# Chains between engines cut into hops one or two rows apart, and a sigmoid made by tanh

## The chip, the cores and the metric

The kernel runs on one core of a Trainium2 chip. The metric is device time in microseconds (us) of one execution. The engines are TensorE (PE), VectorE (DVE), ScalarE (ACT), GpSimd (POOL, which issues the gathers) and SyncE (SP, which issues the plain loads).

## What is computed

A decoder trunk of two layers on 256 tokens of width 1024, all in fp32. Layer 0 mixes with dilated attention (8 heads) and a spatial gating unit (SGU), layer 1 with an S5 state-space layer and a GLU. Each layer ends with PEER: every token picks 8 x 16 = 128 experts of 16384 and adds up their outputs.

```python
h = rmsnorm(x, norm_mix_g[layer])
x = x + hybrid_ab(...)            # layer 0: attention and SGU, one projection in, one out
x = x + s5_block(...)             # layer 1; its end:
    out = g * jax.nn.sigmoid(g @ glu_w + glu_b)        # g = gelu(y), y from the scan of the states
h = rmsnorm(x, norm_ffn_g[layer])
x = x + peer(...)
    sc = einsum('thpc,pkc->thpk', q, subkeys)          # q = h @ wq; top 16 of 128, twice; top 16 of 256 pairs
    act = gelu(einsum('td,tkd->tk', xb, u_tab[ib]))
    y = einsum('tk,tkd->td', gate * act, v_tab[ib])
return rmsnorm(x, final_norm_g)
```

## The kernel before

The 256 tokens are two tiles of 128 (t = 0, 1), one token on each partition. The expert work is 512 rows g: 2 layers x 2 tiles x 128 experts of each token. A row gathers for each of 128 tokens one expert's u and v (8 KB a token, 1 MB a row) into one of RING = 8 buffers. Then dot_product (VectorE, L1189) multiplies u with h and sums; weights (ScalarE, L572 to L578) takes the Gelu of two rows' dots, multiplies them with their gates and writes two diagonal matrices; expert (TensorE, L813) adds the diagonal times v into PSUM. POOL may gather row g once expert(g - 8) is done (L395 to L399). Rows are counted in groups of 16 (n = g // 16), a group for each head, tile and layer; a slot (n, s) is row 16 n + s.

All other work is put between these rows. There is no scheduler: each engine has its own program, made from the same lists. PRELUDE comes ahead of row 0; between() (L80 to L134) puts stages into slots of WORK; LAST comes after row 511. In row g every engine first runs its own functions of that name for the stages in the slot, then its expert work: VectorE a step of the router in the slots of ROUTE and dot_product(g), ScalarE gate_exp in slot EXP_AT and weights(g - 1) in odd rows, TensorE expert(g - 2) and expert(g - 1) in even rows. Each engine executes strictly in its order, and a function waits on semaphores of the engines it reads from. A stage such as q_turn has a function for TensorE (four transposes, L619) and one for VectorE (copy of the result, L974), and both stand in the same slot.

What is put there: query(n, slot, phase, b) makes queries and scores of two heads (q_mm: eight products of 512 columns, L627; q_in: ScalarE copies them, L468; q_turn; q_score: four products with the keys on TensorE, L734, and ScalarE's copy, L478); the second tile's attention, SGU and output projection in groups 1 to 3; the norms (norm, norm_T); for each tile in layer 1 the S5 layer, 16 pairs five rows apart (s5), then s5_end, gate_T and glu. In s5 VectorE makes for each pair the products with the tables of cosines and sines (L1050, L1051), two sums, four scans (L1059) and two more products (L1062, L1063). The tables are made once for two pairs: turn_counts on ScalarE (L500, L502), fraction on VectorE (L1037), tables on ScalarE (L509 to L513). The router of the next group takes five steps, route_keys to route_gate. The functions of Sqrt, Exp, Sin, Sigmoid and the tanh form of Gelu need table loads on ScalarE between them (ACT_TABLE_LOAD rows). SP issues the loads of weights in its own fixed order; each waits until the last product on its buffer is counted in w_used.

## Time and profile before

| what | us |
|---|---|
| median of 3 runs | 1711.5 |
| lowest and highest | 1708.9, 1713.86 |
| the profiled execution | 1707.23 |
| its span, first to last instruction | 1705.5 |
| TensorE busy | 1372.2 (80%) |
| VectorE busy | 1141.1 (67%) |
| ScalarE busy | 671.5 (39%) |
| POOL busy | 567.9 (33%) |
| moved by the transfers | 607.18 MB, mean 356 GB/s |

All views are of the profiled execution, and their times are counted from its first instruction. A busy share says how much of the time an engine computed, not whether it set the pace; for that one reads which wait ended last in each stretch. The dots of row 0 begin at 107.4 us, the first S5 pair of tile 0 at 577 us and of tile 1 at about 989 us.

### The profile page before, as it was taken

The page shows a single profiled execution, that of the slowest core. Times are in us where ns is not written, and L with a number is a line of the kernel's source. Part 1 is how long each engine was busy: PE and PEld are TensorE (multiplying, and loading weights), DVE is VectorE, ACT ScalarE, POOL GpSimd, SP SyncE. Part 2 cuts the span into 40 slices and gives each one's busy share as a digit, 9 for nine tenths or more (in the row PEclk, how much of TensorE's full clock was granted, in tenths as well). Part 3 has the DMA queues.
Part 4 walks back from the last instruction along what each step waited for, and adds up shares of the span by engine and source line. Part 5 has one row for each costly group of instructions (what it writes and reads, how often), then busy time and mean ns, then how long its engine had stood idle before and what let it go on. Part 6 is the DMA issues. An engine that isn't in the chain of part 4 may idle for free.

```text
span 1705.5 us, 14417 instructions
## 1 busy us (share of the span) xinstructions
PE 1372.2 (80%) x3816; PEld 638.7 (37%) x3816; DVE 1141.1 (67%) x2821; ACT 671.5 (39%) x1833; POOL 567.9 (33%) x517
## 2 busy tenths in 40 slices
PE   7997878688797588888878778888978977777776
PEld 3543433233343244444334334444434433222222
DVE  3347563566765799999465589999846556666764
ACT  2224332333333555554243365555334333333332
POOL 0024222233343243444233334333414335434341
PEclk9999889899899798998999989988989999999999
DMA  9479788799899789999999968999989889999996
GB/s 360 174 270 389 290 353 303 304 344 399 334 418 417 286 346 385 360 378 369 373 365 399 384 264 337 366 369 374 371 343 373 341 313 420 421 421 422 422 421 263
DMA packets 106401, 607.18 MB, mean 356 GB/s; under 512 B 9296, under 2 KB 9424, under 8 KB 40784
## 3 DMA queue, kind: packets, MB, share of 16 engines
q0 software_dynamic: 73728, 536.90, 78.9%
q1 hardware_dynamic: 32592, 69.37, 11.1%
q8 instruction: 30, 0.49, 0.1%
q14 instruction: 51, 0.42, 0.1%
HBM read 605.19 MB, written 1.05 MB: 355 GB/s over the span
## 4 chain that ended last, share of the span: by engine, by line
PE 38%; DVE 28%; DMA 17%; DVEq 6%; ACT 6%; issue 4%; ACTq 1%; POOL 0%; POOLq 0%
PE ps L813 23%; DMA rings<-in_uv_tab_dram,idx 16%; PE ps L627 13%; DVE rings L1189 12%; DVE mem L1059 2%; ACT dgs L578 2%; DVEq L1052 1%; ACT wgt L575 1%; DVE mem L1062 1%; DVE mem L1050 1%; PE ps L619 1%; DVEq L1067 1%; DVE mem L1051 1%; ACT gel L572 1%; ACTq L576 1%
## 5 line engine op out<-in xcount | busy, mean ns | idle before, releaser
L813 PE MATMUL ps<-rings,dgs 128*128 128x512 f32 x2048 | 1002.5, 641 | 277.9 <-ACT dgs L578 277.8
L397 POOL DMA_INDIRECT rings<-in_uv_tab_dram,idx x512 | 566.6, 1107 | 1072.4 <-PE ps L813 985.8
L1189 DVE CUSTOM_DVE_ANT_0 rings<-rings,h 128x1024 f32<-128x1024 f32 x512 | 610.9, 1222 | 156.6 <-DMA rings<-in_uv_tab_dram,idx 143.3
L813 PEld LDWEIGHTS ps<-rings,dgs 128*128 128x128 f32 x2048 | 403.5, 204 | 825.5 <-issue 442.2
L572 ACT ACTIVATE gel<-dots 128x2 f32<-128x2 f32 x256 | 52.0, 203 | 651.5 <-DVE dots L1189 651.4
L578 ACT ACTIVATE dgs<-cst,wgt 128x128 f32<-128x128 f32 x512 | 177.6, 394 | 18.8 <-issue 1.4
L627 PE MATMUL ps<-wst,hT 128*128 128x512 f32 x384 | 171.1, 593 | 0.0
L575 ACT ACTIVATE wgt<-gel,share 128x1 f32<-128x1 f32 x512 | 123.0, 287 | 18.0 <-issue 0.3
L974 DVE COPY mem<-ps 128x512 f32<-128x512 f32 x16 | 11.1, 691 | 151.2 <-PE ps L619 151.2
L627 PEld LDWEIGHTS ps<-wst,hT 128*128 128x128 f32 x384 | 72.9, 190 | 92.5 <-issue 91.0
L572 ACT ACT_TABLE_LOAD x60 | 77.0, 1283 | 11.7 <-DVE dots L1189 10.1
L777 PE MATMUL ps<-mem 128*128 128x32 f32 x512 | 62.7, 277 | 0.0
L777 PEld LDWEIGHTS ps<-mem 128*128 128x128 f32 x512 | 59.9, 192 | 5.3 <-issue 1.9
L627 PE MATMUL ps<-rings,hT 128*128 128x512 f32 x128 | 58.5, 608 | 2.0 <-DVE scr L877 1.2
L468 ACT ACTIVATE mem<-ps 128x512 f32<-128x512 f32 x16 | 9.6, 597 | 121.8 <-PE ps L627 121.8
L1189 DVE DVE_READ_ACCUMULATOR2_ANT dots<- 128x1 f32 x512 | 42.0, 82 | 0.0
L559 ACT ACT_TABLE_LOAD x32 | 41.1, 1283 | 0.6
L627 PEld LDWEIGHTS ps<-rings,hT 128*128 128x128 f32 x128 | 24.4, 196 | 31.0 <-issue 30.9
L859 DVE TENSOR_TENSOR x<-x,ps 128x512 f32<-128x512 f32 x12 | 7.9, 683 | 40.3 <-PE ps L627 35.0
L1111 DVE TENSOR_TENSOR mem<-ps,vec 128x512 f32<-128x512 f32 x4 | 2.8, 691 | 42.6 <-PE ps L627 42.6
L1059 DVE TENSOR_TENSOR_SCAN mem<-s5s,z_init,mem 128x128 f32<-128x128 f32 x64 | 25.8, 464 | 1.8 <-issue 0.4
L734 PE MATMUL ps<-sk,mem 128*128 128x128 f32 x128 | 18.2, 286 | 9.4 <-DVE mem L974 9.4
(174 smaller groups left out, 924.4 us busy)
## 6 DMA issues: line engine op xcount, KB each, us to landing
wst<-in_wq_dram SPq DMA_DIRECT2D x15, 2048.0 KB, 10.6
wst<-in_w_out_dram SPq DMA_DIRECT2D x4, 2048.0 KB, 17.2
rings<-in_uv_tab_dram,idx POOLq DMA_INDIRECT x512, 9.6
wst<-in_glu_w_dram SPq DMA_DIRECT2D x4, 2048.0 KB, 22.8
rings<-in_w_in_dram SPq DMA_DIRECT2D x3, 2048.0 KB, 16.6
vec<-in_vecs_dram SPq DMA_DIRECT2D x11, 512.0 KB, 9.0
rings<-in_w_in_dram SPq DMA_DIRECT2D x2, 1024.0 KB, 8.6
dgs<-in_w_in_dram SPq DMA_DIRECT2D x1, 2048.0 KB, 19.4
```

The source lines that it names most:

```text
L397: nc.gpsimd.indirect_dma_start(out=ring[:, g % RING, :], out_offset=None, in_=uv_tab, in_offset=bass.IndirectOffsetOnAxis(ap=idx[n % 4][:, ...
L559: A.activation(gexp[n % 2][:, :], cs[n % 2][:, :], ACT.Exp, bias=ncs[n % 2][:, :], accum_out=gsum[n % 2][:, :]).then_inc(exp_ok, 1)
L572: A.activation(gel[i][:, every], dots[i][:, every], ACT.Gelu_apprx_tanh)
L575: A.activation(wgt[i][:, c], gel[i][:, c], ACT.Copy, scale=share[i][:, c])
L576: act.drain()
L578: A.activation(diag[:, (g + k) % DIAGS, :], ident, ACT.Copy, scale=wgt[i][:, c]).then_inc(diag_ok, 1)
L627: ins = PE.matmul(ps[:, bank, :], lhs[:, k, :], rhs[:, k, :], start=(k == 0), stop=(k == KC - 1))
L734: ins = PE.matmul(ps[:, 2, a * P:(a + 1) * P], qT[:, a, :], sk[:, p // T, a % 2, :], start=True, stop=True)
L777: ins = PE.matmul(o, d, m[:, j, v, :], start=(q == 0), stop=(q == 3))
L813: ins = PE.matmul(ps[:, 4 + 2 * t + b, :], diag[:, g % DIAGS, :], ring[:, g % RING, D + b * BANK:D + (b + 1) * BANK], start=(g % (PH * TOP ...
L1059: V.tensor_tensor_scan(zst[:, i, r, :], dec[:, tile:tile + 1].to_broadcast([P, P]), by_cos[:, i, r, :], z_init[:, r, tile:tile + 1] if t e ...
L1189: V.tensor_tensor_reduce(out=u, in0=u, in1=h[:, t, :], scale=1.0, scalar=0.0, op0=ALU.mult, op1=ALU.add, accum_out=dots[n % 2][:, s:s + 1] ...
```

## The change

Every stage that ran over several engines in one slot is cut at each change of engine, and the parts stand one or two rows apart: query now takes eight rows (q_in one row behind the last product, then q_turn, q_copy, q_score, q_keep), norm six, attention seven. w_out and glu are issued in parts of three or four products (w_mm, glu_mm) as the query's were. Scores go into PSUM bank 3 instead of 2, so that queries can stand five rows apart (slots 107 + 5 b) and overlap. s5 becomes s5_mm, s5_rot, s5_turns, s5_scan and s5_tables in five rows that follow one another; fraction moves to the end of s5_scan. The router's steps and gate_exp move by one slot. y_sum of a tile moves from slot 4 to slot 2. The Sqrt on a spare value ahead of each norm stays only in the prelude. The sigmoid is (1 + tanh(x / 2)) / 2: Tanh on ScalarE, and the 1 and the 0.5 go into the two operations of VectorE that were there. Ring, gathers, dot_product, weights and expert stay as they are.

```diff
 DIAGS = 16
-ROUTE = {2: "route_keys", 4: "route_pairs", 6: "route_best", 8: "route_index", 10: "route_gate"}
-EXP_AT = 8
+ROUTE = {3: "route_keys", 5: "route_pairs", 7: "route_best", 9: "route_index", 11: "route_gate"}
+EXP_AT = 9
 S5_TILES = 32
 RMS_EPS, LN_EPS = 1e-6, 1e-5
...
     def query(n, slot, phase, b):
         at(n, slot, ("q_mm", phase, b, 0, 3))
         at(n, slot + 1, ("q_mm", phase, b, 3, 6))
-        at(n, slot + 2, ("q_mm", phase, b, 6, 8), ("q_in", phase, b))
-        at(n, slot + 3, ("q_turn", phase, b))
-        at(n, slot + 4, ("q_score", phase, b))
-
-    at(0, 0, ("z_out", 6), ("z", 7, 0, 8), ("z_out", 7), ("z", 8, 0, 8), ("z_out", 8), ("z", 9, 0, 8), ("z_out", 9))
-    at(0, 4, ("qk_turn", 1))
+        at(n, slot + 2, ("q_mm", phase, b, 6, 8))
+        at(n, slot + 3, ("q_in", phase, b))
+        at(n, slot + 4, ("q_turn", phase, b))
+        at(n, slot + 5, ("q_copy", phase, b))
+        at(n, slot + 6, ("q_score", phase, b))
+        at(n, slot + 7, ("q_keep", phase, b))
+
+    def norm(n, slot, m):
+        for i, name in enumerate(("norm_sq", "norm_ms", "norm_sd", "norm_h", "norm_T", "hT_copy")):
+            if m < 8 or i < 4:
+                at(n, slot + i, (name, m))
+
+    def product(n, slot, name, *which):
+        at(n, slot, (name, *which, 0, 3))
+        at(n, slot + 1, (name, *which, 3, 6))
+        at(n, slot + 2, (name, *which, 6, 8))
+
+    def attention(n, slot, a):
+        for i, name in enumerate(("att_scores", "att_max", "att_exp", "att_den", "att_pT", "att_pT_copy", "att_o")):
+            at(n, slot + i, (name, a))
+
+    at(0, 0, ("z_out", 6), ("z", 7, 0, 8), ("z", 8, 0, 8), ("z", 9, 0, 8), ("z_out", 7), ("z_out", 8), ("z_out", 9))
+    at(0, 2, ("qk_turn", 1))
+    at(0, 3, ("qkT_copy", 1))
     query(0, 6, 0, 1)
-    at(1, 1, ("sgu_a", 1))
-    at(1, 4, ("att_a", 1))
-    at(1, 6, ("att_b", 1))
-    query(1, 10, 0, 2)
-    at(2, 2, ("att_a", 2))
-    at(2, 4, ("att_b", 2))
-    at(2, 6, ("sgu_b", 1))
-    at(2, 9, ("mix", 1))
-    at(2, 11, ("mix_T", 1))
-    at(2, 13, ("w_out", 1, 0))
-    at(3, 2, ("w_out", 1, 1))
-    at(3, 6, ("norm", 3))
-    at(3, 9, ("norm_T", 3))
-    query(3, 11, 0, 3)
-    query(4, 3, 1, 3)
+    at(1, 1, ("sgu_var", 1))
+    at(1, 2, ("sgu_sd", 1))
+    at(1, 3, ("sgu_norm", 1))
+    at(1, 4, ("sgu_mm", 1))
+    at(1, 5, ("sgu_gate", 1))
+    attention(1, 6, 1)
+    query(1, 13, 0, 2)
+    attention(2, 6, 2)
+    at(2, 14, ("mix", 1))
+    at(2, 15, ("mix_T", 1))
+    at(3, 0, ("mixT_copy", 1))
+    product(3, 1, "w_mm", 1, 0)
+    at(3, 4, ("w_sum", 1, 0))
+    product(3, 4, "w_mm", 1, 1)
+    at(3, 7, ("w_sum", 1, 1))
+    norm(3, 8, 3)
+    query(3, 14, 0, 3)
+    query(4, 4, 1, 3)
     at(5, 2, ("s5_angle",))
     query(5, 8, 1, 0)
     at(6, 2, ("s5_setup",))
     query(6, 9, 1, 1)
-    query(7, 6, 1, 2)
+    query(7, 5, 1, 2)
     for t in range(T):
         g = PH * (t + 1)
-        at(g, 4, ("y_sum", 2 + 2 * t), ("norm", 4 + 2 * t))
-        at(g, 7, ("norm_T", 4 + 2 * t))
+        at(g, 2, ("y_sum", 2 + 2 * t))
+        norm(g, 3, 4 + 2 * t)
         for pair in range(S5_TILES // 2):
-            at(g, 10 + 5 * pair, ("s5", t, pair))
-        at(g, 92, ("s5_end", t))
-        at(g, 94, ("gate_T", t))
-        at(g, 95, ("glu", t, 0))
-        at(g, 99, ("glu", t, 1))
-        at(g, 103, ("norm", 5 + 2 * t))
-        at(g, 106, ("norm_T", 5 + 2 * t))
-        query(g, 108, 2 + t, 0)
-        query(g, 114, 2 + t, 1)
-        query(g, 120, 2 + t, 2)
-        query(g, 128, 2 + t, 3)
-    at(24, 4, ("y_sum", 6), ("norm", 8))
+            slot = 9 + 5 * pair
+            at(g, slot, ("s5_mm", t, pair))
+            at(g, slot + 1, ("s5_rot", t, pair))
+            at(g, slot + 2, ("s5_turns", t, pair))
+            at(g, slot + 3, ("s5_scan", t, pair))
+            at(g, slot + 4, ("s5_tables", t, pair))
+        at(g, 89, ("s5_last", t))
+        at(g, 90, ("s5_sum", t))
+        at(g, 91, ("s5_gelu", t))
+        at(g, 92, ("gate_T", t))
+        at(g, 93, ("gT_copy", t))
+        for b in range(2):
+            at(g, 94 + 2 * b, ("glu_mm", t, b, 0, 4))
+            at(g, 95 + 2 * b, ("glu_mm", t, b, 4, 8))
+            at(g, 96 + 2 * b, ("glu_bias", t, b))
+            at(g, 97 + 2 * b, ("glu_sig", t, b))
+            at(g, 98 + 2 * b, ("glu_sum", t, b))
+        norm(g, 101, 5 + 2 * t)
+        for b in range(4):
+            query(g, 107 + 5 * b, 2 + t, b)
+    at(24, 2, ("y_sum", 6))
+    norm(24, 3, 8)
     return work
...
-            def norm(m):
+            def warm():
+                A.activation(sq_warm[:, :], half_pi, ACT.Sqrt)
+
+            def norm_sq(m):
                 t = NORM_T[m]
                 if m < 2:
                     act.wait_ge(ld_x[t], 16)
                 else:
-                    A.activation(sq_warm[:, :], half_pi, ACT.Sqrt)
                     act.wait_ge(x_done, 2 * (m - 1))
                 A.activation(h[:, t, :], x[:, t, :], ACT.Square, accum_out=ss[:, t:t + 1]).then_inc(sq_done, 1)
+
+            def norm_sd(m):
+                t = NORM_T[m]
                 act.wait_ge(ms_done, m + 1)
                 A.activation(sd[:, t:t + 1], ms[:, t:t + 1], ACT.Sqrt).then_inc(sd_done, 1)
...
-            def q_score(p, b):
+            def q_keep(p, b):
...
-                A.activation(S[:, cols, :], ps[:, 2, :].rearrange("p (a s) -> p a s", a=2),
+                A.activation(S[:, cols, :], ps[:, 3, :].rearrange("p (a s) -> p a s", a=2),
                              ACT.Copy).then_inc(s_act, 1)
...
-            def s5(t, pr):
+            def s5_mm(t, pr):
+
+                if pr == 0:
+                    act.wait_ge(hT_act, 5 + 2 * t)
+                    turn_counts(KC * t)
+                    tables(KC * t)
+
+            def s5_turns(t, pr):
 
                 c = pr // 2
                 ci = KC * t + c
                 if pr % 2:
-                    if c + 1 < KC:
-                        tables(ci + 1)
...
+            def s5_tables(t, pr):
+
+                if pr % 2 and pr + 1 < 16:
+                    tables(KC * t + pr // 2 + 1)
...
-            def glu(t, b):
+            def glu_sig(t, b):
                 act.wait_ge(bias_ok, 2 * t + b + 1)
                 g = gate[:, b * BANK:(b + 1) * BANK]
-                A.activation(g, g, ACT.Sigmoid).then_inc(sig_ok, 1)
+                A.activation(g, g, ACT.Tanh, scale=0.5).then_inc(sig_ok, 1)
...
 
-            def w_out_(t, b):
-                pe.wait_ge(mT_act, t + 1)
-                pe.wait_ge(mT_dve, t + 1)
-                banks_2_3()
-                stream(2 + b, t, WOUT_USE[t] + b)
+            def w_mm(t, b, k0, k1):
+                if k0 == 0:
+                    pe.wait_ge(mT_act, t + 1)
+                    pe.wait_ge(mT_dve, t + 1)
+                    banks_2_3()
+                stream(2 + b, t, WOUT_USE[t] + b, k0, k1)
 
             def q_mm(p, b, k0, k1):
                 if k0 == 0:
...
                 turn(3, qs, qt_done)
+                moved["qs"] = (qs_act, k + 1)
 
             def q_score(p, b):
 
                 pe.wait_ge(qt_dve, k + 1)
                 pe.wait_ge(ld_sk, 16)
                 for a in range(4):
-                    ins = PE.matmul(ps[:, 2, a * P:(a + 1) * P], qT[:, a, :], sk[:, p // T, a % 2, :], start=True, stop=True)
+                    ins = PE.matmul(ps[:, 3, a * P:(a + 1) * P], qT[:, a, :], sk[:, p // T, a % 2, :], start=True, stop=True)
                 ins.then_inc(s_done, 1)
                 moved["scores"] = (s_act, k + 1)
 
...
+            def s5_scan(t, pr):
+
+                c, js, cos, sin, by_cos, by_sin = s5_views(pr)
...
+                V.tensor_tensor(by_cos, zst, cos, ALU.mult).then_inc(d_ok, 1)
+                V.tensor_tensor(by_sin, zst, sin, ALU.mult).then_inc(d_ok, 1)
...
+                dve.drain()
                 if pr % 2 and pr + 1 < 16:
-                    fraction(ci + 1)
-                s5_pair(t, pr)
-
-            def s5_end(t):
+                    fraction(KC * t + c + 1)
+
...
+            def glu_sum(t, b):
+                cols = slice(b * BANK, (b + 1) * BANK)
                 dve.wait_ge(sig_ok, 2 * t + b + 1)
-                V.tensor_tensor(gate[:, cols], gate[:, cols], h[:, t, cols], ALU.mult)
-                dve.drain()
-                residual(t, b, gate[:, cols])
+                V.scalar_tensor_tensor(gate[:, cols], gate[:, cols], 1.0, h[:, t, cols], ALU.add, ALU.mult)
+                dve.drain()
+                xs = x[:, t, cols]
+                V.scalar_tensor_tensor(xs, gate[:, cols], 0.5, xs, ALU.mult, ALU.add).then_inc(x_done, 1)
```

## Rows read from the trace of the kernel before

**Rows 1.** The page: transfers in 40 equal slices of the span

```profile
...
DMA  9479788799899789999999968999989889999996
GB/s 360 174 270 389 290 353 303 304 344 399 334 418 417 286 346 385 360 378 369 373 365 399 384 264 337 366 369 374 371 343 373 341 313 420 421 421 422 422 421 263
```

**Rows 2.** Windows: length; PE, PEld, DVE, ACT, POOL busy (count); clock, DMA share, GB/s

```profile
...
107.40:571.60 464.20, 363.15 (x920) 167.71 (x919) 275.65 (x708) 159.85 (x440) 150.53 (x138) 0.92 0.91 359
...
603.00:809.90 206.90, 180.61 (x621) 92.31 (x620) 194.88 (x490) 106.26 (x298) 84.97 (x73) 0.90 0.93 366
809.90:984.10 174.20, 142.84 (x373) 66.06 (x372) 93.81 (x232) 61.35 (x158) 52.29 (x48) 0.95 0.97 380
...
1015.90:1233.00 217.10, 186.75 (x650) 95.63 (x649) 201.18 (x483) 108.79 (x306) 86.19 (x76) 0.91 0.92 363
1233.00:1413.10 180.10, 149.82 (x366) 67.40 (x364) 97.87 (x242) 65.09 (x171) 57.63 (x51) 0.93 0.91 346
1413.10:1691.00 277.90, 205.44 (x445) 80.09 (x446) 184.31 (x456) 94.00 (x301) 110.22 (x107) 1.00 1.00 417
```

**Rows 3.** Waits, whole span: us in total, times, longest one

```profile
...
POOL rings L397 <- PE ps L813: 985.8, 451, 16.0
...
DVE mem L974 <- PE ps L619: 151.2, 16, 13.4
...
ACT mem L468 <- PE ps L627: 121.8, 16, 13.4
...
DVE mem L1111 <- PE ps L627: 42.6, 4, 12.3
```

**Rows 4.** Timelines of VectorE, ScalarE, TensorE around one query: start, us, what, idle before

```profile
...
369.96 0.69 DVE L974 COPY mem<-ps 128x512 f32<-128x512 f32 x1 [12.35 <-PE ps L619]
...
368.61 0.60 ACT L468 ACTIVATE mem<-ps 128x512 f32<-128x512 f32 x1 [13.36 <-PE ps L627]
...
358.11 5.31 PE L627 MATMUL ps<-wst,hT 128*128 128x512 f32 x12
363.26 3.60 PE L813 MATMUL ps<-rings,dgs 128*128 128x512 f32 x8
```

**Rows 5.** Timeline of TensorE in the stretch of gathers alone, two experts

```profile
...
1669.17 3.70 PE L813 MATMUL ps<-rings,dgs 128*128 128x512 f32 x8 [1.26 <-ACT dgs L578]
```

**Rows 6.** Waits of VectorE from 620 to 780 us, inside the first S5 stretch

```profile
...
DVE rings L1189 <- DMA rings<-in_uv_tab_dram,idx: 1.4, 2, 1.2
```

**Rows 7.** Timelines of ScalarE and VectorE inside the first S5 stretch

```profile
...
678.70 0.20 ACT L572 ACTIVATE gel<-dots 128x2 f32<-128x2 f32 x1 [1.15 <-DVE dots L1189]
...
680.24 1.28 ACT L509 ACT_TABLE_LOAD   x1
681.53 0.63 ACT L509 ACTIVATE mem<-mem 128x512 f32<-128x512 f32 x1
...
682.75 0.72 ACT L512 ACTIVATE mem<-mem,cst 128x512 f32<-128x512 f32 x1
...
685.60 1.22 DVE L1189 CUSTOM_DVE_ANT_0 rings<-rings,h 128x1024 f32<-128x1024 f32 x1
...
686.75 1.22 DVE L1189 CUSTOM_DVE_ANT_0 rings<-rings,h 128x1024 f32<-128x1024 f32 x1
```

**Rows 8.** Timeline of VectorE at the first S5 pair

```profile
...
577.42 0.69 DVE L1037 SCALAR_TENSOR_TENSOR mem<-mem 128x512 f32<-128x512 f32 x1 [3.45 <-ACT mem L502]
580.74 0.69 DVE L1050 TENSOR_TENSOR mem<-ps,mem 128x512 f32<-128x512 f32 x1 [2.63 <-ACT mem L512]
```

**Rows 9.** Timeline of VectorE, start of route_best and the dot behind it

```profile
...
370.56 0.42 DVE L1146 MAX8 cs<-cand_a 128x8 f32<-128x256 f32 x1
...
373.35 1.23 DVE L1189 CUSTOM_DVE_ANT_0 rings<-rings,h 128x1024 f32<-128x1024 f32 x1
```

**Rows 10.** Timeline of ScalarE at the end of the kernel

```profile
...
1700.27 0.19 ACT L413 ACTIVATION_READ_ACCUMULATOR h<-x 128x1 f32 x1
1700.67 0.20 ACT L415 ACTIVATE sd<-ms 128x1 f32<-128x1 f32 x1 [0.22 <-DVE ms L844]
```

More of the change, by code:

```diff
@@ L520, in s5 @@
                 if pr % 2:
-                    if c + 1 < KC:
-                        tables(ci + 1)
                     return
-                if c == 0:
-                    act.wait_ge(hT_act, 5 + 2 * t)
-                    turn_counts(ci)
-                    tables(ci)
-                    if t == 0:
-                        act.wait_ge(ld_c, 16)
-                        act.wait_ge(cz_zero, 2)
+                if c == 0 and t == 0:
+                    act.wait_ge(ld_c, 16)
+                    act.wait_ge(cz_zero, 2)
                 if c + 1 < KC:
@@ L684, in att_b, with att_o @@
                     turn(2 + i, E[i], pT_done)
+                moved["pT"] = (pT_act, 2 * a + 2)
+            def att_o(a):
+                t, units = att_units(a)
                 for i, (h0, nh) in enumerate(units):
```

144 lines of the change are left out of this document (80 added, 64 removed).

## The prediction

> **What bounds the kernel now.** I read the 40 slices first, then the windows by stretch, then the waits, then the timelines. The main loop is 512 rows, and each row gathers 1 MB. In the last stretch the chip moves 417 GB/s at a DMA share of 1.00, and single slices show 421 or 422 [rows 1, 2]. Nothing but gathers and expert work is left there, so this is the ceiling of the transfers. Everywhere else one asks what keeps the kernel below it. The windows split the loop into two kinds. The two S5 stretches (603.0 to 809.9 and 1015.9 to 1233.0) have VectorE busy for 194.9 of 206.9 us and 201.2 of 217.1 us, and in 160 us of the first VectorE waited only 1.4 us for gathered rows [rows 2, 6]: VectorE is the bound, its small gaps are bubbles. The three other stretches have VectorE at 54 to 59%, TensorE at 78 to 83%, and the transfers at 359, 380 and 346 GB/s [rows 2]: no engine is full, and waits across engines are what costs. The waits name them: POOL waits 985.8 us for TensorE to free a ring buffer, VectorE waits 151.2 us in 16 places for a transposed query, ScalarE 121.8 us for the same 16 query products, VectorE 42.6 us in 4 places for the GLU products [rows 3].
>
> **Why those waits reach the transfers.** Before, the stages of a chain stand in one row or in two neighbouring ones of every engine's order. TensorE's work of a row stands ahead of the experts of the two rows before, so it is late by some rows. A VectorE that has reached the row stands still until TensorE comes. The query at 358 shows it: VectorE idles 12.35 us for the transpose; ScalarE idles 13.36 us before it copies the product, and so holds back the weights of dots that were finished when VectorE fell idle (369.96 - 12.35 = 357.6); TensorE needs 5.31 us for six of the eight products and 3.60 us for two experts in between [rows 4]. With no new weights no expert runs, no buffer is freed, no gather starts.
>
> **Part 1, the stretches outside S5.** Moved by the gathers' ceiling, the bytes of the three stretches (464.2 x 359, 174.2 x 380, 180.1 x 346) would take 396, 157 and 148 us, 117 us less than they do. By the DMA share (0.91, 0.97, 0.91) they were idle for 42, 5 and 16 us, together 63. The first counts the less efficient weight loads as loss, the second misses half-empty queues. I take the middle, 90 us, as what could be recovered. How much is? In the free rhythm a row takes 2.5 us, and two experts 3.70 us on TensorE [rows 2, 5]. For a query that starts in an even row, take the end of the dot of the row before as zero. TensorE is free at about 0; three products (2.65 us), a pair of experts (3.7), three products, the last two (1.9) put the end of q_mm at about 11 us, the next pair's at 14.5 and the transpose's near 15.3. ScalarE, whose next weights need the dot that ends at 10, copies the product then: late by about 1 us instead of idling 7.6 (121.8 / 16). VectorE gets to q_copy at 12.5 and waits about 3 us instead of 9.4 (151.2 / 16). What lasts is TensorE itself: a query is 7.2 us of products and some 2 us of transposes and scores, in 5 rows that leave 12.5 - 5 x 1.85 = 3.2 us. Where four queries stand 5 rows apart (slots 107 to 129) TensorE is the local bound at (5 x 1.85 + 9.2) / 5 = 3.7 us a row, and the 2 MB of weights of each query cost the transfers nearly as much. y_sum moves from slot 4 to slot 2, where the last experts of the tile are just finished, and can wait some us behind such a cluster, three times. So I take three quarters of the 90, **68 us**; the ends are a third (30), if these clusters rule, and all of the high figure (117).
>
> **Part 2, the first S5 pair of each tile.** Before, VectorE waits 3.45 us for turn_counts and 2.63 us for tables [rows 8]. After, ScalarE makes the counts one row ahead, and its table load too. What remains is about 2 us of Sin, Abs and Sin, so 2 x (3.45 + 2.63 - 2) = **8 us** for both tiles; the price is that the weights of slots 8 and 9 stand behind that row of ScalarE, ends 0 and 12.
>
> **Part 3, the later S5 tables.** This one goes the other way. Before, ScalarE makes the next tables in the row where VectorE first makes the fraction and then a whole pair and five dots, so nobody waits. Now the fraction stands at the end of s5_scan (slot + 3), tables at slot + 4, and the s5_rot that reads them at the next slot + 1, only three dots on. The slots with tables are 14, 24 ... 74, all even, so slot + 3 is odd and ScalarE first makes the weights of that row, which need its dot. From the start of that dot: 1.23 until its result, 0.1, weights 1.54 (678.70 to 680.24), table load 1.29, Sin, Abs, Sin 1.94: 6.1 us. VectorE is there after three dots of 1.15, at 3.45 [rows 7]. That is a stall of 2.65 us on the engine that is the bound, seven times a tile, 18.6. A router step between the dots hides some: route_best (373.35 - 370.56 = 2.8 us [rows 9]) one whole stall, route_keys and route_pairs by their sizes about 1.7 each, route_gate 0.4. That leaves 18.6 - 2.65 - 3.4 - 0.4 = 12 a tile, **24 us lost**. The ends are 0 (VectorE is itself held up elsewhere) and 14 x (2.65 + 3.6) = 87 us: the weights of the next pair are queued behind the tables and a reload, TensorE's experts wait for them 3.6 us longer (until 7.4 instead of 3.8), and that is added if it starves the ring as well. The split of the pair itself adds no instruction, and I cost it at nothing, since VectorE has its landed rows anyway.
>
> The Trainium skill (page "ScalarE: Activation LUTs", section "What ACT_TABLE_LOAD costs") puts a switch at about 2.66 us, load and drain together. Here Sin starts 0.01 us after a load of 1.28 us ended [rows 7], so the trace disagrees and the row decides; by the page the stalls would be 1.4 us longer each and the sum 19 us worse.
>
> **Part 4, small edits.** The prelude has the same order on each engine; its rows cost nothing. The warm Sqrt goes, except once: its load moves to norm_sd. In the loop the count of loads stays. At the end it was made while ScalarE waited for the last sum, now it stands between Square and Sqrt (1700.46 to 1700.67), and costs 1.28 - 0.21 = **1.1 us** [rows 10]. Sigmoid by Tanh removes up to 8 table loads of 1.28 us if Tanh is in the set of the Gelu, none if not; both are beside TensorE's product, so 0, ends 0 and 5 gained. Scores in bank 3 let the next product start early: part of the 68. The router one row later: the index is still ready before the expert whose buffer that gather takes, nothing. Attention, SGU and norms in hops belong to part 1. SP's queue keeps its order; its loads wait for w_used and h_done and come earlier or later with them.
>
> **Sum.** -68 - 8 + 24 + 1 = -51 us. Against the profiled execution's 1707.2 us that is 1656; the median of the three runs is 4.3 us above the profiled one, so the forecast is 1711.5 - 51, **1660 us**.
>
> **The rivals.** (B) The transfers become the bound nearly everywhere and VectorE's S5 stalls are half as large: -90 - 8 + 12 + 1 = -85, **1626 us**. For it: the stretch from 1413 runs at 417 GB/s as soon as no chains cross. (C) One row is too short a distance: TensorE is late by two rows in the clusters, so every hop is a wait again, and only 40% of 90 returns: -36 - 8 + 24 + 1 = -19, **1692 us**. For it: TensorE at 83% of the last such stretch; against: a row there is 3.3 us, which leaves more room. (D) Slower: tables in S5. If a table costs the full 6.25 us, then -68 - 8 + 87 + 1 = +12, **1723 us**; it decides from (68 + 8 - 1) / 14 = 5.4 us a table. For it: a DVE-bound stretch pays every wait in full; against: the ring holds eight rows. (E) The change doesn't decouple: engines meet later in the same order and wait as long, **1711 us**. Against: TensorE's late row is one or two rows late, as the pairs of experts in the query's rows show, and the new distances are as long. (F) A table switch costs about twice its load (14 x 1.4 us of further stall): 19 us on top of the forecast, **1679 us**; the trace speaks against it [rows 7]. That is what the Trainium skill's rule above would give.
>
> **Chances.** Forecast 0.50, B 0.18, C 0.19, D 0.06, E 0.05, F 0.02. Within 0.3% (5 us) is what a measurement of this kernel can't tell from no change. Faster 0.90, same 0.04, slower 0.06. The forecast's own range is 1640 to 1680; the wide one goes from 1615 (all of B) to 1700 (all of C).
>
> **What would show it.** In the profile after: VectorE's wait for the transpose before q_copy falls from 9.4 us to about 3 each; the share of the transfers in the first stretch rises to about 0.97; the S5 stretches stay as long or get some 8 us longer each, with a new VectorE wait for the Sin of tables, 2 to 3 us in about five of seven rows; a table load before the last Sqrt. The prediction is wrong if S5 itself gets shorter (then VectorE wasn't the bound), or if POOL's wait for TensorE stays near 986 us with TensorE busy throughout (then TensorE was).

## The result and the profile after

| what | us |
|---|---|
| before, median of 4 runs on the same chip | 1710.44 |
| after, median of 4 runs (lowest, highest) | 1660.04 (1657.36, 1663.61) |
| ratio after / before, 95% interval | 0.9704 (0.9680 to 0.9728) |
| the profiled execution of after, and its span | 1663.61, 1661.6 |

The change is 50.4 us faster by the medians; the two profiled executions are 43.6 us apart, since the profiled one of after is the slowest of its four. The forecast was 1660, with a range of 1615 to 1700.

The first view is again the page's slices of transfers, which [rows 1] show for before.

```profile
...
DMA  9569799999799999888999999989899899999996
GB/s 360 188 254 400 315 377 368 407 393 391 324 400 417 366 370 343 333 348 347 384 412 367 413 363 359 340 311 343 355 385 399 315 402 421 422 421 421 413 414 257
```

Outside S5 the slices are fuller: the seventh to ninth have 368, 407 and 393 where before had 303, 304 and 344. The ceiling is where it was, 421 to 422. The windows by stretch (length; PE, PEld, DVE, ACT, POOL busy with counts; clock, DMA share, GB/s) are cut at the dots of rows 0, 136, 146, 218, 264, 274, 348, 400 and 511, as in [rows 2].

```profile
...
107.40:535.90 428.50, 354.36 (x917) 163.19 (x915) 274.36 (x699) 151.12 (x430) 152.59 (x138) 0.93 0.96 380
535.90:565.00 29.10, 21.26 (x75) 10.55 (x76) 25.29 (x56) 18.16 (x52) 8.74 (x8) 0.82 0.88 345
565.00:789.40 224.40, 187.62 (x642) 94.16 (x641) 198.89 (x500) 114.09 (x311) 83.27 (x75) 0.92 0.91 353
789.40:942.90 153.50, 135.81 (x350) 62.70 (x348) 88.68 (x222) 52.54 (x145) 49.26 (x46) 0.93 0.99 392
942.90:971.70 28.80, 20.91 (x75) 10.40 (x76) 26.28 (x59) 17.21 (x47) 10.82 (x8) 0.82 0.87 352
971.70:1202.00 230.30, 189.61 (x651) 95.64 (x650) 203.29 (x493) 115.62 (x313) 88.20 (x77) 0.92 0.90 347
1202.00:1367.30 165.30, 144.79 (x365) 65.26 (x363) 97.93 (x243) 60.05 (x169) 58.42 (x53) 0.96 0.95 375
1367.30:1646.70 279.40, 212.04 (x446) 83.54 (x447) 184.76 (x456) 93.92 (x301) 111.38 (x107) 0.97 1.00 415
```

VectorE's work in the first line is what it was (274.4 against 275.7 us busy), so nearly all of the 35.7 us that went was time in which it stood idle; TensorE's idle time fell by 27 us there. In the S5 lines VectorE's busy time grew by 4.0 and 2.1 us while the lengths grew by 17.6 and 13.2 us.

The same stretches for the kernels that follow, in us, each read off the dots of its own trace. Each line is one execution. Up to row 136 after, e1, e2, e6 and e11 are the same program, and there they have 421.5 to 432.7 us; in the first cluster (218-264) e6 and e11, the same program up to the last row, have 152.1 and 145.4. So a difference of less than some 10 us in the first column, or 7 in a cluster, says little by itself:

| kernel | 0-136 | 136-146 | S5 146-218 | 218-264 | 264-274 | S5 274-348 | 348-400 | 400-511 | last dot to end |
|---|---|---|---|---|---|---|---|---|---|
| before | 464.2 | 31.4 | 206.8 | 174.2 | 31.8 | 217.1 | 180.2 | 278.3 | 14.1 |
| after | 428.5 | 29.2 | 224.4 | 153.5 | 28.8 | 230.3 | 165.3 | 279.4 | 14.9 |
| e3, S5 hops alone | 465.1 | 28.1 | 217.3 | 173.9 | 28.3 | 227.8 | 180.1 | 278.1 | 14.1 |
| e4, query hops alone | 463.2 | 31.4 | 206.7 | 165.7 | 31.9 | 215.9 | 167.7 | 278.5 | 14.1 |
| e5, all but S5 and query hops | 439.0 | 32.5 | 214.6 | 156.1 | 32.8 | 220.0 | 168.9 | 278.7 | 14.9 |
| e2, all but S5 hops | 432.7 | 32.6 | 214.4 | 157.6 | 32.9 | 218.8 | 168.9 | 279.3 | 14.9 |
| e1, after with early fraction | 425.1 | 29.0 | 212.3 | 151.5 | 29.2 | 218.5 | 166.7 | 279.1 | 14.9 |
| e6, e1 with last query later | 428.0 | 28.6 | 213.2 | 152.1 | 28.8 | 217.7 | 158.0 | 279.2 | 14.9 |
| e10, e6 with the copy a row later | 425.9 | 28.5 | 211.7 | 148.7 | 28.8 | 217.5 | 158.3 | 277.9 | 14.9 |
| e11, e6 with the Sqrt ahead of the end | 421.5 | 28.5 | 212.6 | 145.4 | 29.1 | 217.6 | 159.8 | 277.0 | 13.8 |
| e12, all that helped | 422.0 | 28.7 | 211.8 | 144.3 | 29.5 | 217.7 | 158.1 | 279.0 | 13.8 |

The waits of after over the whole span (engine, line, waited for: us in total, times, longest):

```profile
...
POOL rings L434 <- PE ps L869: 942.8, 459, 19.9
...
DVE rings L1264 <- DMA rings<-in_uv_tab_dram,idx: 173.5, 132, 4.3
...
DVE mem L1041 <- PE ps L668: 104.0, 16, 16.3
...
ACT mem L510 <- PE ps L676: 89.9, 16, 13.5
...
DVE mem L1182 <- PE ps L676: 32.4, 4, 10.2
...
DVE mem L1137 <- issue: 24.1, 12, 2.6
...
PE ps L676 <- DMA wst<-in_wq_dram: 12.8, 2, 7.8
```

The waits of [rows 3] are smaller, not gone: VectorE's for the transposed query 104.0 us instead of 151.2, ScalarE's for the query's product 89.9 instead of 121.8, VectorE's for GLU's product 32.4 instead of 42.6. Two are new: VectorE 12 times at L1137 (the first product with the tables) for 24.1 us, and TensorE twice for weights of a query. Eleven of the twelve, 22.8 us, stand in the two S5 stretches at tables that come late; the twelfth, 1.28 us at 950.86, is at the first pair of the second tile. Here is one of the twelve, in timelines of ScalarE and VectorE from 596 us (start, us, what, idle before):

```profile
...
597.36 0.20 ACT L620 ACTIVATE gel<-dots 128x2 f32<-128x2 f32 x1 [4.65 <-DVE dots L1264]
...
598.89 1.28 ACT L551 ACT_TABLE_LOAD   x1
600.18 0.63 ACT L551 ACTIVATE mem<-mem 128x512 f32<-128x512 f32 x1
...
601.40 0.72 ACT L554 ACTIVATE mem<-mem,cst 128x512 f32<-128x512 f32 x1
...
602.21 0.69 DVE L1137 TENSOR_TENSOR mem<-ps,mem 128x512 f32<-128x512 f32 x1 [2.60 <-issue]
```

ScalarE makes the weights of the odd row first (597.36), then loads the table, then makes the Sin; VectorE starts its product 0.1 us after the last Sin ends and has stood still for 2.60 us. The profile puts the wait down to "issue"; that it is the Sin is seen by setting the two engines side by side, and e1 tests it.

### The profile page after: what moved, and what is told of

It is laid out like the page before. It is cut to its first block and busy times, and to the rows that moved or that the text cites. A ratio compares the mean times of both kernels' runs of the same rounds, so it can differ in the third digit from the quotient of the medians.

```text
span 1661.6 us, 14475 instructions
## 1 busy us (share of the span) xinstructions
PE 1366.6 (82%) x3816; PEld 634.4 (38%) x3816; DVE 1142.9 (69%) x2821; ACT 654.3 (39%) x1814; POOL 568.5 (34%) x517
## 5 line engine op out<-in xcount | busy, mean ns | idle before, releaser
L1264 DVE CUSTOM_DVE_ANT_0 rings<-rings,h 128x1024 f32<-128x1024 f32 x512 | 615.5, 1224 | 190.3 <-DMA rings<-in_uv_tab_dram,idx 173.5
L620 ACT ACTIVATE gel<-dots 128x2 f32<-128x2 f32 x256 | 52.0, 203 | 684.5 <-DVE dots L1264 684.1
L676 PE MATMUL ps<-wst,hT 128*128 128x512 f32 x384 | 176.6, 606 | 14.5 <-DMA wst<-in_wq_dram 12.8
L1041 DVE COPY mem<-ps 128x512 f32<-128x512 f32 x16 | 11.1, 692 | 104.0 <-PE ps L668 104.0
L620 ACT ACT_TABLE_LOAD x54 | 69.3, 1283 | 1.7
L510 ACT ACTIVATE mem<-ps 128x512 f32<-128x512 f32 x16 | 9.6, 597 | 89.9 <-PE ps L676 89.9
L1137 DVE TENSOR_TENSOR mem<-ps,mem 128x512 f32<-128x512 f32 x32 | 22.0, 689 | 26.4 <-issue 24.1
L607 ACT ACT_TABLE_LOAD x30 | 38.5, 1283 | 0.7
L918 DVE TENSOR_TENSOR x<-x,ps 128x512 f32<-128x512 f32 x12 | 7.9, 684 | 36.9 <-PE ps L676 24.6
L1182 DVE TENSOR_TENSOR mem<-ps,vec 128x512 f32<-128x512 f32 x4 | 2.8, 692 | 32.4 <-PE ps L676 32.4
## 6 DMA issues: line engine op xcount, KB each, us to landing
wst<-in_glu_w_dram SPq DMA_DIRECT2D x4, 2048.0 KB, 23.7
rings<-in_w_in_dram SPq DMA_DIRECT2D x3, 2048.0 KB, 16.6
```

The lines of the kernel that those rows point to most:

```text
L607: A.activation(gexp[n % 2][:, :], cs[n % 2][:, :], ACT.Exp, bias=ncs[n % 2][:, :], accum_out=gsum[n % 2][:, :]).then_inc(exp_ok, 1)
L620: A.activation(gel[i][:, every], dots[i][:, every], ACT.Gelu_apprx_tanh)
L676: ins = PE.matmul(ps[:, bank, :], lhs[:, k, :], rhs[:, k, :], start=(k == 0), stop=(k == KC - 1))
L1041: V.tensor_copy(qT, four(3)).then_inc(qt_dve, 1)
L1137: V.tensor_tensor(by_cos, x4, cos, ALU.mult)
L1264: V.tensor_tensor_reduce(out=u, in0=u, in1=h[:, t, :], scale=1.0, scalar=0.0, op0=ALU.mult, op1=ALU.add, accum_out=dots[n % 2][:, s:s + 1] ...
```

## The experiments

**e1: the fraction early, the tables two rows earlier.** It tells whether the waits for late tables cost their full length, and whether they are the distance's fault.

```diff
-            at(g, slot + 4, ("s5_tables", t, pair))
+            at(g, slot + 2, ("s5_tables", t, pair))
...
             def s5_rot(t, pr):
...
+                if pr % 2 and pr + 1 < 16:
+                    fraction(KC * t + c + 1)
...
             def s5_scan(t, pr):
...
-                if pr % 2 and pr + 1 < 16:
-                    fraction(KC * t + c + 1)
```

> The changed kernel with one thing moved: fraction goes from the end of s5_scan to the end of s5_rot (odd pairs), and s5_tables from slot + 4 to slot + 2, so that ten rows lie between the tables and the s5_rot that reads them. Theory (part 3 of the prediction: VectorE is the bound in S5 and each late table costs 2.6 us): the 12 waits before the first product of s5_rot (24.1 us after the change) go, and the time falls by 20 to 24 us, to 1636 to 1640. Rival (the waits only took the place of other idle time, since transfers and the ring would have held VectorE up anyway): the waits go, waits for gathered rows come in their place, and the time falls by less than 8 us.

Measured: 1636.62 us, 0.9578 (0.9550 to 0.9607) of before, 23.4 less than after. The eleven waits for late tables are gone; what is left is the one at the first pair of the second tile, whose tables the edit doesn't touch:

```profile
...
DVE mem L1137 <- issue: 1.3, 1, 1.3
```

The windows of its S5 stretches:

```profile
...
562.70:775.00 212.30, 177.12 (x640) 90.70 (x639) 198.10 (x500) 109.66 (x307) 88.12 (x74) 0.95 0.94 370
...
955.70:1174.20 218.50, 183.12 (x653) 93.62 (x652) 202.89 (x491) 110.97 (x308) 89.14 (x77) 0.95 0.94 365
```

They are 12.1 and 11.8 us shorter with VectorE nearly as busy as in after: 22.8 us of waits for tables and 1.6 us that it stands less at s5_sum, against 23.9 us of time. The waits for gathered rows that the rival expected in their place did not come (170.7 us over the span, 173.5 in after). In S5 these waits of VectorE cost their whole length.

**e2: the hops of S5 taken back, the rest of the change kept.** The five stages of a pair stand in one slot again, with the fraction ahead of the pair.

```diff
-            at(g, slot, ("s5_mm", t, pair))
...
-            at(g, slot + 4, ("s5_tables", t, pair))
+            for name in ("s5_mm", "s5_rot", "s5_turns", "s5_scan", "s5_tables"):
+                at(g, 10 + 5 * pair, (name, t, pair))
```

> The changed kernel with the S5 pairs put back into one row each (slot 10 + 5 per pair; fraction ahead of the pair, tables beside it), everything else as changed. Theory (the split of a pair is worth nothing, only its tables cost): the first pair of each tile costs about 4 us more again and the late tables are gone, so 8 us above the kernel with the early fraction: 1644 to 1648, and 12 to 16 us below the changed kernel. Rival (two short visits of VectorE instead of one long one help the ring): well above the kernel with the early fraction, 1655 or more.

Measured: 1649.47 us, 0.9645 (0.9610 to 0.9680); its profiled execution was the longest of four, 1661.09. By the median it is 10.6 us faster than after: the hops of S5, as the change has them, lose time. It is 12.9 us slower than e1, which has the hops of after with an early fraction. So the hops are worth something once the fraction isn't late: in the profiles the stretches 136-146 and 264-274, with the first pair in them, are 3.6 and 3.7 us shorter in e1. The rest lies mostly outside S5, in rows where the two are the same program, so it isn't shown that the hops give it.

**e3: the hops of S5 alone, on the kernel before.**

```diff
-            at(g, 10 + 5 * pair, ("s5", t, pair))
+            slot = 9 + 5 * pair
+            at(g, slot, ("s5_mm", t, pair))
...
+            at(g, slot + 4, ("s5_tables", t, pair))
```

> The kernel before with only the S5 pairs in hops, as the changed kernel has them; queries, norms, attention, GLU as before. Theory: slower than before by the sum of parts 2 and 3, 24 - 8 = 16 us, 1724 to 1730. Rival (hops in S5 gain, and the changed kernel's long S5 stretches come from something else, such as the router one row later): 1711 or less.

Measured: 1721.91 us, 1.0074 (1.0046 to 1.0103), 13.8 slower than the 1708.12 of before beside it, a little less than the theory's 16. Of its waits, the one at its first product with the tables:

```profile
...
DVE mem L1081 <- issue: 23.7, 12, 2.6
```

Twelve waits for late tables, six in each tile, without anything else of the change. By stretch: +10.5 and +10.7 in S5, -3.3 and -3.5 at the first pairs, together +14.4. That is parts 2 and 3 of the prediction measured alone (it had -8 and +24).

**e4: the hops of the queries alone, on the kernel before** (with scores in bank 3 and the first query of a cluster at slot 107).

```diff
-        at(n, slot + 2, ("q_mm", phase, b, 6, 8), ("q_in", phase, b))
-        at(n, slot + 3, ("q_turn", phase, b))
-        at(n, slot + 4, ("q_score", phase, b))
+        at(n, slot + 2, ("q_mm", phase, b, 6, 8))
+        at(n, slot + 3, ("q_in", phase, b))
+        at(n, slot + 4, ("q_turn", phase, b))
+        at(n, slot + 5, ("q_copy", phase, b))
+        at(n, slot + 6, ("q_score", phase, b))
+        at(n, slot + 7, ("q_keep", phase, b))
```

> The kernel before with only the queries in hops (eight rows, scores in bank 3), started in the slots of before (the first of a cluster one slot earlier, because its scores must be kept in time); norms, attention, output projection, GLU and S5 as before. Theory (queries' waits were 151 of the about 280 us that VectorE waited outside S5): about half to two thirds of the gain of the stretches outside S5 (85 us by the marks of the rows), 40 to 55 us, 1655 to 1670. Rival (the gain came from the norms, attention and y_sum around them): under 20 us, above 1690.

Measured: 1683.55 us, 0.9848 (0.9819 to 0.9877), 24.6 us faster than before, between what the theory (40 to 55) and the rival (under 20) expected. Its wait for the transposes:

```profile
...
DVE mem L980 <- PE ps L623: 78.5, 14, 13.7
```

72.7 us of waits are gone, and the stretches give -8.5 and -12.5 in the two clusters and only -1.0 in rows 0 to 136, where seven of the 15 queries stand. It fits that the chains of attention, SGU and norms, still in one row each, held the engines up there anyway (e5).

**e5: all but the hops of S5 and of the queries** (e2, with each query in its five rows of before, and the clusters at 108, 114, 120, 128; the slots of y_sum and the router, and Tanh, are those of after).

```diff
-        at(n, slot + 2, ("q_mm", phase, b, 6, 8))
-        at(n, slot + 3, ("q_in", phase, b))
-        at(n, slot + 4, ("q_turn", phase, b))
-        at(n, slot + 5, ("q_copy", phase, b))
-        at(n, slot + 6, ("q_score", phase, b))
-        at(n, slot + 7, ("q_keep", phase, b))
+        at(n, slot + 2, ("q_mm", phase, b, 6, 8), ("q_in", phase, b))
+        at(n, slot + 3, ("q_turn", phase, b), ("q_copy", phase, b))
+        at(n, slot + 4, ("q_score", phase, b), ("q_keep", phase, b))
...
-            query(g, 107 + 5 * b, 2 + t, b)
+            query(g, (108, 114, 120, 128)[b], 2 + t, b)
```

> The kernel with S5 pairs in one row, and the queries too put back to five rows and to their old slots (scores stay in bank 3): so only attention, SGU, output projection, norms, GLU and y_sum are in hops. Queries alone gave 25 us, and S5 in one row with all others in hops gave 59. Theory (parts add up, since the stalls stand in different rows): 1708 - (59 - 25) = 1674, 1669 to 1680. Rival (they overlap: a stall taken away in a row only pays once its neighbour is gone too): either half alone gives less than its share, 1685 or more.

Measured: 1663.56 us, 0.9746 (0.9724 to 0.9769), 43.6 us faster than before, more than either theory gave it. Its wait for the transposes is nearly that of before (151.2 us):

```profile
...
DVE mem L1034 <- PE ps L661: 147.0, 16, 16.4
```

So 43.6 us can be had while the waits that the prediction put first are all there. Queries alone give 24.6 and the others alone 43.6, 68.2 in sum, and e2, which has both, gives 58.7: they overlap, mostly in the clusters (218-264: -8.5, -18.1 and together -16.6; 348-400: -12.5, -11.3 and together -11.3). There each edit takes part of what the other would; it isn't a last bound, since e12 gets to 144.3 and 158.1. In rows 0 to 136 it is the other way round: -1.0 and -25.2 alone, together -31.5 in e2 and -35.7 to -42.7 in after, e1, e6 and e11, which are the same program there. So the queries' hops pay in those rows only once the other chains are cut.

**e6: e1 with the last query of a cluster three rows later.**

```diff
-            query(g, 107 + 5 * b, 2 + t, b)
+            query(g, (107, 112, 117, 125)[b], 2 + t, b)
```

> The kernel with the early fraction, and the fourth query of each cluster starts in slot 125 instead of 122. Theory (the waits of 13 to 16 us for its transpose come from weights that land 30 us after their issue, for which TensorE waited 7.8 us in one cluster and 5.1 in the other): TensorE's wait for the weights goes, and 5 to 12 us fall off, 1625 to 1632. Rival (TensorE or the transfers are full over the whole cluster, so the wait only moves): within 3 us of 1637.

Measured: 1627.81 us, 0.9529 (0.9502 to 0.9556), 8.8 us less than e1. What it is aimed at, in after's timelines of TensorE and VectorE in the first cluster:

```profile
...
877.30 2.74 PE L676 MATMUL ps<-wst,hT 128*128 128x512 f32 x6
...
900.28 5.30 PE L676 MATMUL ps<-wst,hT 128*128 128x512 f32 x6 [7.75 <-DMA wst<-in_wq_dram]
...
918.11 0.69 DVE L1041 COPY mem<-ps 128x512 f32<-128x512 f32 x1 [16.31 <-PE ps L668]
```

The load of these weights is issued at 870.18 and takes 30.0 us to land; TensorE stands 7.75 us for it, and VectorE 16.31 us for the transpose behind it. The wait costs TensorE more than its length: the six matmuls behind it take 5.30 us where six took 2.74 just before, and from 900.28 to 904 the granted clock is 0.50, the lower of its two levels (1.2 GHz), after TensorE had stood idle. In e6 the waits, whole span:

```profile
...
DVE mem L1041 <- PE ps L668: 92.0, 16, 12.5
...
PE ps L676 <- DMA wst<-in_wq_dram: 5.1, 1, 5.1
```

In this execution the second cluster is 8.7 us shorter than in e1, and the first isn't: there TensorE now waits 5.1 us for the weights of the third query. It isn't so in every execution: in e11, the same program up to the last row, TensorE waits for no weights, and both clusters are shorter than in e1, by 6.1 and 6.9 us. The medians, 1627.81 and 1622.10 against 1636.62, leave no doubt of the gain.

**e7: Sigmoid in place of Tanh,** on the kernel after.

```diff
-                A.activation(g, g, ACT.Tanh, scale=0.5).then_inc(sig_ok, 1)
+                A.activation(g, g, ACT.Sigmoid).then_inc(sig_ok, 1)
...
-                V.scalar_tensor_tensor(gate[:, cols], gate[:, cols], 1.0, h[:, t, cols], ALU.add, ALU.mult)
+                V.tensor_tensor(gate[:, cols], gate[:, cols], h[:, t, cols], ALU.mult)
```

> The changed kernel with the sigmoid as before (Sigmoid on ScalarE, product and sum as two plain operations). Theory (part 4: the 8 or so table loads stand beside TensorE's product): four loads for Sigmoid and as many for the Gelu come back, the time stays within 3 us of 1660. Rival (each load delays the weights in rows where VectorE waited 10 and 6 us for the GLU product, so both halves pay): 5 to 10 us more, 1665 to 1670.

Measured: 1658.70 us, 0.9695 (0.9672 to 0.9717), no difference to after's 1660.04 that can be measured. ScalarE's groups by line (busy us, mean ns, idle before) in e7:

```profile
...
L620 ACT ACT_TABLE_LOAD x58 | 74.4, 1283 | 5.2 <-DVE dots L1264 3.4
...
L600 ACT ACT_TABLE_LOAD x4 | 5.1, 1283 | 0.1
```

In after there is none at L600, the Tanh, and 54 at L620:

```profile
...
L620 ACT ACT_TABLE_LOAD x54 | 69.3, 1283 | 1.7
```

The eight loads are real, 10.3 us of ScalarE, and what they cost in time can't be measured, as the prediction had it.

**e8: fewer products.** e1, where each query beside the experts leaves out the odd chunks but the last, three of its eight products.

```diff
+                    if half and k % 2 and k != KC - 1:
+                        continue
```

> The kernel with the early fraction, and three of the eight products of each of the 15 queries between the rows left out (so the queries are not the reference's, and other experts are gathered): 15 x 3 x 0.86 = 39 us less work on TensorE, transfers unchanged. Theory of the prediction (TensorE is the local bound where queries stand): 20 to 39 us less, 1598 to 1617. Rival (transfers are the bound by now, TensorE only sets how late VectorE gets its transposes): less than 10 us, above 1627.

**e9: half the weights.** e1, where twelve of those 15 queries load 1 MB instead of 2 MB.

```diff
-                    sp.dma_start(wst[:, w % 2, :, :], m[:, :, n * BANK:(n + 1) * BANK]).then_inc(ld_w[w % 2], 16)
+                    kk = KC // 2 if w > 4 and blocks[w][0] is not w_out and blocks[w][0] is not glu_w else KC
+                    sp.dma_start(wst[:, w % 2, 0:kk, :], m[:, 0:kk, n * BANK:(n + 1) * BANK]).then_inc(ld_w[w % 2], 16)
```

> The kernel with the early fraction, and of the 12 query weight loads that run beside the rows only the first half is loaded (the products read old values for the other half, so the queries are not the reference's): 12.6 MB less, TensorE's work unchanged. At 400 GB/s that is 31 us of transfers. Theory of the prediction (TensorE bounds the clusters): less than 10 us. Rival (the transfers bound them): 20 to 31 us less, 1606 to 1617.

Measured: e8 1619.52 us, 0.9488 (0.9466 to 0.9510), 17.1 less than e1; e9 1616.01 us, 0.9463 (0.9438 to 0.9489), 20.6 less than e1. The windows of the two cluster stretches, of e8:

```profile
...
772.10:920.30 148.20, 123.33 (x327) 57.34 (x325) 89.00 (x223) 52.97 (x146) 47.63 (x46) 0.95 1.00 398
...
1167.60:1324.50 156.90, 132.57 (x341) 60.15 (x339) 97.87 (x244) 60.20 (x169) 57.86 (x53) 0.97 1.00 398
```

and of e9:

```profile
...
774.30:918.30 144.00, 133.13 (x351) 61.71 (x349) 88.72 (x222) 52.92 (x146) 49.64 (x46) 0.96 0.98 382
...
1164.20:1323.20 159.00, 144.43 (x365) 65.21 (x363) 97.58 (x244) 60.20 (x169) 59.20 (x53) 0.97 0.94 368
```

With less work for TensorE (e8) the transfers are full (1.00, 398 GB/s), and TensorE still waits 17.3 us for weights, in two places. With fewer bytes (e9) TensorE is at 92 and 91% of the stretches, and waits for no weights. By the expectations e8's 17.1 us lie between the prediction's theory, that TensorE bounds the clusters, and the rival; e9's 20.6 us lie in the rival's range, that the transfers do. So TensorE alone is not the bound there: each edit gains some and neither gains all. e11, which leaves nothing out, has clusters nearly as short (145.4 and 159.8 us), so what e8 and e9 save is not all work or bytes; part of it is time that better slots save too. What both together would give was not tried.

**e10: the copy one row later,** on e6, for all queries but the first of each cluster.

```diff
+        far = not (phase >= 2 and b == 0)
...
-        at(n, slot + 5, ("q_copy", phase, b))
-        at(n, slot + 6, ("q_score", phase, b))
-        at(n, slot + 7, ("q_keep", phase, b))
+        at(n, slot + 5 + far, ("q_copy", phase, b))
+        at(n, slot + 6 + far, ("q_score", phase, b))
+        at(n, slot + 7 + far, ("q_keep", phase, b))
```

> The kernel with the early fraction and the late fourth query, and q_copy, q_score and q_keep one row later for all queries but the first of each cluster. Theory (one row between q_turn on TensorE and q_copy on VectorE is too short, 92 us of waits in 16 places; a further row of 2.5 to 3.5 us takes that much off each): the waits fall by 30 to 40 us, the time by 5 to 15, 1613 to 1623. Rival (VectorE's waits lie beside transfers that are full there, so they cost nothing): the waits fall, the time stays within 3 us of 1628.

Measured: 1622.78 us, 0.9498 (0.9479 to 0.9517), 5.0 less than e6. Its wait for the transposes:

```profile
...
DVE mem L1042 <- PE ps L669: 51.1, 12, 8.8
```

41 us of waits went (92.0 to 51.1) for 5 us of time at most, and perhaps for none: e11 has e6's slots and e6's waits (89.6 us), and its median is 1622.10 us, 5.7 below e6's, of which the Sqrt accounts for 1.1. Against e6 the 5.0 us are at the lower end of the theory's 5 to 15, against e11 they are the rival's nothing; these runs don't decide. Outside S5 a wait of VectorE is mostly slack, in S5 (e1) none of it is.

**e11: the Sqrt on a spare value again ahead of the last norm,** on e6.

```diff
-LAST = [("y_sum", 7), ("norm_sq", 9), ("norm_ms", 9), ("norm_sd", 9), ("norm_h", 9)]
+LAST = [("y_sum", 7), ("warm",), ("norm_sq", 9), ("norm_ms", 9), ("norm_sd", 9), ("norm_h", 9)]
```

> The kernel with the early fraction and the late fourth query, and a Sqrt on a spare value put back ahead of the last norm. Theory: the table load leaves the chain between the last Square and the last Sqrt; the time from the last dot to the end falls from 14.9 to 13.9 us and the whole by about 1 us, less than rounds can show. Rival (the load is hidden behind VectorE's small step anyway): 14.9 us stays.

Measured: 1622.10 us, 0.9503 (0.9472 to 0.9533). ScalarE's timeline at the end of after

```profile
...
1654.32 1.06 ACT L452 ACTIVATE h<-x 128x1024 f32<-128x1024 f32 x1 [4.82 <-DVE x L918]
1655.28 0.19 ACT L452 ACTIVATION_READ_ACCUMULATOR h<-x 128x1 f32 x1
1655.49 1.28 ACT L457 ACT_TABLE_LOAD   x1
1656.78 0.20 ACT L457 ACTIVATE sd<-ms 128x1 f32<-128x1 f32 x1
```

and of e11:

```profile
...
1602.90 1.28 ACT L444 ACT_TABLE_LOAD   x1
...
1608.67 0.19 ACT L452 ACTIVATION_READ_ACCUMULATOR h<-x 128x1 f32 x1
1609.07 0.20 ACT L457 ACTIVATE sd<-ms 128x1 f32<-128x1 f32 x1 [0.22 <-DVE ms L900]
```

The load has gone under the wait for the last sum, and from the last dot to the end it is 13.8 instead of 14.9 us. In the whole time 1.1 us can't be told from the spread: the medians of e11 and e6 are 5.7 us apart, and so much can lie between two measurements of what is nearly one kernel.

**e12: e1, e6, e10 and e11 together.**

> All that paid, in one kernel: the changed kernel with the early fraction, the fourth query in slot 125, q_copy a row later, and the Sqrt on a spare value ahead of the last norm. Theory (the parts stand in different rows): 1636.6 - 8 - 5 - 1, about 1621 to 1624, a ratio to before of 0.949. Rival (the last row's distance and the late query feed on the same waits): 1627 or more.

Measured over five rounds: 1619.51 us, 0.9484 (0.9459 to 0.9509), against 1708.57 of before beside it. It is 40.5 us faster than after and the best version of those that leave nothing out (e9 is 3.5 us below it with half of those weights unread). By 3 us it can't be told apart from e10 and e11.

## Why the prediction was right, step by step

The mechanisms were right in sign in all four parts. That the median, 1660.04, came out at the forecast is luck beyond that: the two profiled executions, from which the parts are read, are 43.6 us apart where the sum had 51, and the medians 50.4. By stretch, in the profiled executions: part 1, rows 0-136, 218-264 and 348-400, -35.7 - 20.7 - 14.9 = -71 (predicted -68); part 2, -2.2 - 3.0 = -5 (-8); part 3, +17.6 + 13.2 = +31 (+24); the stretch of gathers alone +1.1, the end +0.8 (+1.1).

**Part 1, the size right, the reason half right.** The share of the transfers in the first stretch is 0.96, with 0.97 predicted. The 90 us that the prediction called recoverable are there: e12's three stretches (422.0, 144.3, 158.1) are 94 us shorter than before's. Three quarters of it was a choice, though, and the step under it failed: VectorE's wait for the transpose fell to 6.5 us each (104.0 / 16), not to 3, and ScalarE's for the product to 5.6 (89.9 / 16), not to about 1. The count of rows let TensorE start a query at zero and gave VectorE 2.5 us a row. For the query that starts in row 88, with the end of the dot of row 87 at 386.29 as zero, TensorE's products start at 1.5 us and end at 11.9, and its transposes end at 15.8, near the 11 and 15.3 of the count. But VectorE has done its last dot ahead of q_copy after 9.5 us, not 12.5:

```profile
...
395.70 0.08 DVE L1264 DVE_READ_ACCUMULATOR2_ANT dots<- 128x1 f32 x1
402.13 0.69 DVE L1041 COPY mem<-ps 128x512 f32<-128x512 f32 x1 [6.35 <-PE ps L668]
```

In the clusters TensorE is the late one: its products start 3.1 to 7.4 us after that zero even where it waits for no weights. The count had also left out the load of the weights: it named the transfers' cost of them and then let TensorE have them on time, while in after one came 30.0 us after its issue. That makes the two longest waits, 16.31 and 13.36 us (e6), but it is the smaller part: e11, where TensorE waits for no weights, still has 5.6 us each (89.6 / 16). The prediction also read the queries' waits of [rows 3, 4] as the main thing. By e5 the smaller chains of attention, SGU, norms, GLU and router, which it put in one sentence, give 43.6 us by themselves, and by e4 the queries' 24.6. The list of waits ranks chains by how long somebody stands, and that isn't what they cost: 41 us of such waits were worth 5 at most (e10). y_sum in slot 2 waits as it had said, 3.64 us in two of three places.

**Part 2, right, slightly too large.** The two waits of [rows 8] became one of 2.08 us, at the first product with the tables:

```profile
...
543.82 0.69 DVE L1137 TENSOR_TENSOR mem<-ps,mem 128x512 f32<-128x512 f32 x1 [2.08 <-ACT mem L554]
```

That is 3.45 + 2.63 - 2.08 = 4.0 us, as predicted, and in the second tile 3.44 + 1.84 - 1.28 = 4.0; of it 2.2 and 3.0 us arrive in after, and 3.3 and 3.5 in e3.

**Part 3, the stalls nearly to the tenth, the stretches more.** Predicted were stalls of 2.65 us less what the router hides, 12 us a tile and 24 in sum. Measured alone (e3) they are three of 2.60, one of 2.22, of 0.98 and of 0.85 us in each tile, 23.7 in sum; in after the 0.85 is missing in the first tile, and the sum is 22.8. Their removal gives 23.4 us back (e1). The other 8 us by which the two stretches grew (30.8 - 22.8) are not the tables: with the fraction early they are still 5.5 and 1.4 us longer than before in e1, and 7.6 and 1.7 in e2, where a pair's stages stand in one row. The rows of VectorE on both sides say what they are. s5_sum stands in slot 90, ahead of the dot of row 218 that ends the first stretch, where before it stood in slot 92, behind it: 2.5 us of work and a wait of 3.40 us come into the stretch, as a shift of the mark. In the second tile, whose stretch ends at the dot of row 348, it stood ahead of the mark before as well, and its wait is 3.08 us instead of 2.95. And with the router one row later each stretch holds 1.5 to 1.9 us more of VectorE's router work. With the stalls that makes 18.4 and 13.8 us, where 17.6 and 13.2 were measured. e3, where neither was moved, grows by 21.2 us, no more than its stalls.

**Part 4, right.** The Sqrt's load stands at 1655.49 between Square and Sqrt and costs 1.1 us (e11); the sigmoid is worth nothing that can be measured (e7). Over the kernel ScalarE has 121 table loads instead of 133; eight of the twelve are the sigmoid's (129 in e7), and four more fell, where the prediction had the loop's count stay.

**The rivals.** B (1626, S5's stalls half as large) is refuted for this kernel by the eleven waits for late tables; e12 comes under its time by another way, without them. C (1692) saw the lasting waits in the clusters rightly, but they aren't paid in full; the 3.3 us a row that it gives for the last of them is 180.1 / 52 = 3.5. D (1723, 6.25 us a table) fell: over its 14 tables the cost is 1.7 us each (23.7 / 14). In e3, where nothing covers it, the kernel does get slower, by 13.8 us: the stalls that [rows 7] give, less what the first pairs gain, and no starved ring on top. E fell with the result. F fell too: in the timeline above Sin starts at 600.18, 0.01 us after the load that began at 598.89 ends, and the stall is 2.60 us, where twice the load would have made it 4.0. The Trainium skill (page "ScalarE: Activation LUTs", section "What ACT_TABLE_LOAD costs") gives about 2.66 us a switch, about 1283 ns of it for the load. The load's part is what the rows have (1283 ns on average in e7 and in after), the drain's part no row of this case shows.

## What to carry to other kernels

Ask of every wait what its engine is in that stretch. Where the engine is the bound (VectorE in S5), a wait costs its full length (22.8 us of waits, 23.4 us of time), and a chain that is stretched over rows must have its producer early enough by the count of what stands between; elsewhere the same engine's waits were worth an eighth of their length at most (e10). When chains are cut into hops, cost the loads that feed them too, and don't give the waiting engine its mean time a row: it arrives early where its data have landed. Measure the same rows in several executions before reading a few us out of a stretch, and expect edits that attack the same bound to overlap: 24.6 and 43.6 us alone made 58.7 together.

## What the runs showed of the hardware

The same loads of 2 MB took longer after the change, when the transfers beside them were fuller. The page's groups of DMA issues (KB each, median us from issue to landing) of before:

```profile
...
wst<-in_wq_dram SPq DMA_DIRECT2D x15, 2048.0 KB, 10.6
```

and of after:

```profile
...
wst<-in_wq_dram SPq DMA_DIRECT2D x15, 2048.0 KB, 18.6
```

The one in the first cluster took 30.0 us. A buffer of weights that was early enough in before was late twice in after. Fullness isn't the whole of it: e11, with its first cluster at 403 GB/s, has a median of 17.8 us, and e1, with 402, one of 21.3.

